# The scan's input products from a stack of 96 rows: one fp32r pass each in place of full fp32

## The reference, cut to what matters

```python
h = rms_norm(x, attn_norm_g[i])
proj = h @ w_in[i] + b_in[i]
q, k, v, u, gate_attn, gate_ssm = jnp.split(proj, SPLIT_POINTS, axis=-1)
...
ug = u.reshape(bsz, l, SSM_GROUPS, SSM_GROUP)          # 32 groups of 16 channels
...
bu_re = jnp.einsum('gph,blgh->blgp', bb_re, ug)        # 64 states of each group
bu_im = jnp.einsum('gph,blgh->blgp', bb_im, ug)
...
_, _, xs_re, xs_im = lax.associative_scan(combine, (a_re_t, a_im_t, bu_re, bu_im), axis=1)
y = (jnp.einsum('ghp,blgp->blgh', c_re, xs_re) - jnp.einsum('ghp,blgp->blgh', c_im, xs_im)
     + d_skip.reshape(SSM_GROUPS, SSM_GROUP) * ug)
```

## Time and profile before

| | |
|---|---|
| time before, median of 3 runs | 2671.86 us (2671.49 to 2672.24) |
| profiled execution, span from first to last instruction | 2672.7 us |
| PE busy | 2642.9 us (99%) |
| DVE busy | 1804.4 us (68%) |
| ACT busy | 1274.7 us (48%) |
| POOL busy | 249.9 us (9%) |
| granted TensorE clock, mean over the span | 0.995 |

### The profile page before, as it was taken

The page is one execution under the profiler, slowest core; times in us unless marked ns, Lnnn a source line. Parts: engine busy times, 40 slices in busy tenths (PEclk is TensorE's granted clock), DMA queues, the critical chain, the costliest instruction groups (busy, mean ns, idle before and its releaser), DMA issues.

```text
span 2672.7 us, 57540 instructions
## 1 busy us (share of the span) xinstructions
PE 2642.9 (99%) x22834; PEld 2628.9 (98%) x22834; DVE 1804.4 (68%) x2269; ACT 1274.7 (48%) x1548; POOL 249.9 (9%) x206
## 2 busy tenths in 40 slices
PE   9999999999999999999999999999999999999998
PEld 9999999999999999999999999999999999999998
DVE  5455555747888888864467999867576777775444
ACT  5334455345344444444455556554455555554442
POOL 1000000030000000001101665400100000000000
PEclk9999999999999999999999999999999999999999
DMA  7665556574555655556656555556656666666664
GB/s 256 193 199 175 150 161 182 169 213 148 173 195 196 196 194 189 196 191 203 192 168 200 174 163 157 155 183 200 194 183 195 196 194 193 191 190 197 195 191 141
DMA packets 137806, 496.71 MB, mean 186 GB/s; under 512 B 15425, under 2 KB 15425, under 8 KB 137537
## 3 DMA queue, kind: packets, MB, share of 16 engines
q1 hardware_dynamic: 137520, 494.20, 59.7%
q10 hardware_dynamic: 144, 0.52, 0.1%
HBM read 492.57 MB, written 2.10 MB: 185 GB/s over the span
## 4 chain that ended last, share of the span: by engine, by line
PE 89%; DVE 6%; DVEq 2%; ACT 1%; DMA 1%; issue 1%; ACTq 0%; SPq 0%
PE bank L432 86%; DVE w_lo L982 2%; PE ps_a L432 1%; PE ps_o L432 1%; PE ps_n L432 1%; DVE act_lo L1021 1%; PE ps_t L432 0%; DMA hT<-in_xT 0%; ACT w_hi L676 0%; DMA w_raw<-in_w_in 0%; ACT act_hi L742 0%; DVE hT L1046 0%; DVE pr L1309 0%; DVE rstd L1005 0%; DVEq L1299 0%
## 5 line engine op out<-in xcount | busy, mean ns | idle before, releaser
L982 DVE TENSOR_TENSOR w_lo<-w_raw,w_hi 128x1024 fp32r<-128x1024 f32 x928 | 1134.1, 1234 | 720.8 <-ACT w_hi L676 719.2
L676 ACT ACTIVATE w_hi<-w_raw 128x1024 fp32r<-128x1024 f32 x928 | 977.0, 1056 | 1185.9 <-PE bank L432 1045.3
L432 PE MATMUL bank<-act_hi,w_hi 128*128 128x256 f32 x5408 | 1275.3, 279 | 3.0 <-DVE gate_y L1350 2.5
L432 PE MATMUL bank<-act_lo,w_hi 128*128 128x256 f32 x5408 | 1264.9, 277 | 0.0
L432 PEld LDWEIGHTS bank<-act_hi,w_hi 128*128 128x128 f32 x5408 | 1014.9, 188 | 4.1 <-issue 2.7
L432 PEld LDWEIGHTS bank<-act_lo,w_hi 128*128 128x128 f32 x5408 | 1015.7, 188 | 0.7
L432 PE MATMUL bank<-act_hi,w_lo 128*128 128x256 f32 x5408 | 726.9, 277 | 2.7 <-DVE w_lo L982 2.7
L432 PEld LDWEIGHTS bank<-act_hi,w_lo 128*128 128x128 f32 x5408 | 666.6, 188 | 3.1 <-DVE w_lo L982 3.1
L432 PE MATMUL bank<-f_lo,w_hi 128*128 128x256 f32 x1408 | 327.9, 276 | 0.0
L432 PE MATMUL bank<-f_hi,w_hi 128*128 128x256 f32 x1408 | 327.9, 276 | 0.0
L432 PEld LDWEIGHTS bank<-f_lo,w_hi 128*128 128x128 f32 x1408 | 264.3, 188 | 0.0
(11 more groups left out here) (227 smaller groups left out, 1790.3 us busy)
## 6 DMA issues: line engine op xcount, KB each, us to landing
w_raw<-in_w_up SPq DMA_DIRECT2D x352, 512.0 KB, 4.2
w_raw<-in_w_in SPq DMA_DIRECT2D x252, 512.0 KB, 4.2
w_raw<-in_w_down SPq DMA_DIRECT2D x176, 512.0 KB, 4.2
w_raw<-in_w_out SPq DMA_DIRECT2D x64, 512.0 KB, 4.4
w_raw<-in_w_ple_gate SPq DMA_DIRECT2D x32, 512.0 KB, 4.5
w_raw<-in_w_branch_attn SPq DMA_DIRECT2D x16, 512.0 KB, 3.9
w_raw<-in_w_branch_a SPq DMA_DIRECT2D x8, 512.0 KB, 4.1
w_raw<-in_w_branch_b SPq DMA_DIRECT2D x8, 512.0 KB, 3.5
```

Of the source, the lines that this page charges most:

```text
L432: return pe.matmul(o, l, r, start=start, stop=stop, skip_group_check=True)
L676: act.activation(w_hi[:, k, 0:n, :], w_raw[:, k, 0:n, :], ACT.Copy).then_inc(hi_ready, 1)
L982: dve.tensor_tensor(w_lo[:, k, 0:n, :], w_raw[:, k, 0:n, :], w_hi[:, k, 0:n, :].bitcast(F32), ALU.subtract).then_inc(lo_ready, 1)
```

## The change

The products of a scan tile have 32 rows that are not zero. The host now lays B's 32 rows three times into bc_pad, at partitions 0, 32 and 64, with nothing below. Three DMAs issued by ACT bring the 32 channels of u to the same three places of u_raw. ACT rounds both to fp32r into stack, 96 rows of B and 96 of u. DVE then replaces the rows of B from 64 and the rows of u from 32 by what rounding took off. So the 96 rows hold high, high and low B beside high, low and high u, and one fp32r product over 96 rows gives the three partial sums that a piece's products also use. C and everything behind the products stays.

Where this stands is set by three new place functions. The fetch (at_fetch) of tiles 0 and 1 is behind ACT's piece 10, of later ones behind piece max(13, 4n+4). The rounding on ACT and the subtractions on DVE (at_stack) are behind their pieces 11 and 13 for tiles 0 and 1, then 4n+7. PE's products (at_input) are behind piece 10 and 14 for tiles 0 and 1, then 4n+8 as before. The queues of SP and POOL hold what they held.

```diff
--- before.py
+++ after.py
@@ -61,6 +61,10 @@
 at_stick = lambda h: 43 + 6 * h
 at_state = lambda n: 8 + 4 * n
 at_head = lambda h: 22 + 3 * h
+
+at_fetch = lambda n: 10 if n < 2 else max(13, 4 * n + 4)
+at_stack = lambda n: (11, 13)[n] if n < 2 else 4 * n + 7
+at_input = lambda n: (10, 14)[n] if n < 2 else at_state(n)
 
 
 def which(place, count, n):
@@ -226,6 +230,8 @@
         pT2_buf = tab[:, 0:BLK]
         vtok = tab[:, 2 * BLK:2 * BLK + T].rearrange("p (k c) -> p k c", k=2)
         turn_t = tab[:, 2 * BLK + T:2 * BLK + 3 * T].rearrange("p (k t) -> p k t", k=2)
+
+        stack, u_raw = over(40 * T, ("stack", [P, 2, 4 * P], F32R), ("u_raw", [P, 2, T]))
 
         x2_hi, x2_lo, glu_v, glu_g = over(
             PROJ2 * T, ("x2_hi", [P, 16, T], F32R), ("x2_lo", [P, 16, T], F32R), ("glu_v", [P, 4, T]), ("glu_g", [P, 4, T]))
@@ -270,6 +276,8 @@
         turns_ready, rot_ready, out_scaled = sem("turns_ready"), sem("rot_ready"), sem("out_scaled")
         negated = sem("negated")
         scans_ready, x_im_ready = sem("scans_ready"), sem("x_im_ready")
+        u_landed = [sem(f"u_landed{i}") for i in range(2)]
+        stack_rounded, stack_ready = sem("stack_rounded"), sem("stack_ready")
         v_ready, v_read, x_ready, x_used = sem("v_ready"), sem("v_read"), sem("x_ready"), sem("x_used")
         y_kept, y_act, ple_used = sem("y_kept"), sem("y_act"), sem("ple_used")
         stored = sem("stored")
@@ -586,16 +594,13 @@
             def mixer_2(n):
                 if n == 3:
                     sum_squares(4)
-                for m in which(at_state, STATE_TILES, n):
-
-                    if m % 8 == 0:
-                        pe.wait_ge(biased_ready, m // 8 + 1)
-                    pe.wait_ge(bc_landed[m % STATE_RING], 16 * (m // STATE_RING + 1))
+                for m in which(at_input, STATE_TILES, n):
+                    pe.wait_ge(stack_ready, m + 1)
                     if m >= 2:
                         pe.wait_ge(v_read, m - 1)
-                    u = proj2[:, U2 + m // STATE_BLOCK, :]
-                    mm(ps_a[m % 2][:, 0:TOK], bc_pad[:, m % STATE_RING, 0, :], u, True, True)
-                    mm(ps_a[m % 2][:, TOK:], bc_pad[:, m % STATE_RING, 1, :], u, False, True).then_inc(v_ready, 1)
+                    u = stack[0:96, m % 2, 2 * P:]
+                    mm(ps_a[m % 2][:, 0:TOK], stack[0:96, m % 2, 0:P], u, True, True)
+                    mm(ps_a[m % 2][:, TOK:], stack[0:96, m % 2, P:2 * P], u, False, True).then_inc(v_ready, 1)
                 for m in which(lambda m: at_state(m) + 6, STATE_TILES, n):
                     k = m % STATE_BLOCK
                     if k == 0 and m:
@@ -832,6 +837,22 @@
                 if n == 7:
                     root(4)
                     act.preload_act_table(ACT.Exp)
+                for m in which(at_fetch, STATE_TILES, n):
+                    act.wait_ge(biased_ready, m // 8 + 1)
+                    if m >= 2:
+                        act.wait_ge(stack_ready, m - 1)
+                    rows = slice(32 * (m % STATE_BLOCK), 32 * (m % STATE_BLOCK) + 32)
+                    for j in range(3):
+                        act.dma_start(u_raw[32 * j:32 * j + 32, m % 2, :], proj2[rows, U2 + m // STATE_BLOCK, :]
+                                      ).then_inc(u_landed[m % 2], 16)
+                for m in which(at_stack, STATE_TILES, n):
+                    act.wait_ge(bc_landed[m % STATE_RING], 16 * (m // STATE_RING + 1))
+                    if m >= 2:
+                        act.wait_ge(v_ready, m - 1)
+                    act.activation(stack[0:96, m % 2, 0:2 * P].rearrange("p (i s) -> p i s", i=2),
+                                   bc_pad[0:96, m % STATE_RING, 0:2, :], ACT.Copy)
+                    act.wait_ge(u_landed[m % 2], 48 * (m // 2 + 1))
+                    act.activation(stack[0:96, m % 2, 2 * P:], u_raw[0:96, m % 2, :], ACT.Copy).then_inc(stack_rounded, 1)
                 for m in which(lambda m: at_state(m) + LEAD - 1, STATE_TILES, n):
                     if m == 0:
                         act.wait_ge(turns_ready, 1)
@@ -1228,6 +1249,11 @@
                     root(4)
                 if n in (4, 5):
                     turn_tables(n - 4)
+                for m in which(at_stack, STATE_TILES, n):
+                    dve.wait_ge(stack_rounded, m + 1)
+                    b, u = stack[64:96, m % 2, 0:2 * P].rearrange("p (i s) -> p i s", i=2), stack[32:64, m % 2, 2 * P:]
+                    dve.tensor_tensor(b, bc_pad[64:96, m % STATE_RING, 0:2, :], b.bitcast(F32), ALU.subtract)
+                    dve.tensor_tensor(u, u_raw[32:64, m % 2, :], u.bitcast(F32), ALU.subtract).then_inc(stack_ready, 1)
                 for step in range(3):
                     for m in which(lambda m: at_state(m) + LEAD + step, STATE_TILES, n):
                         state_tile(m, step)
@@ -1663,7 +1689,8 @@
         vb, vc = np.asarray(v[f"ssm_b_{part}_2"])[0], np.asarray(v[f"ssm_c_{part}_2"])[0]
         for g in range(32):
             ch, st = slice(16 * (g % 8), 16 * (g % 8) + 16), slice(64 * (g % 2), 64 * (g % 2) + 64)
-            bc[ch, g // 2, i, st] = vb[g].T
+            for j in range(3):
+                bc[32 * j + 16 * (g % 2):32 * j + 16 * (g % 2) + 16, g // 2, i, st] = vb[g].T
             bc[st, g // 2, 2 + i, ch] = vc[g].T
     return bc
 
```

## The result

The changed kernel takes 2697.28 us (median of 4 runs, 2695.41 to 2699.28) against 2671.68 for the kernel before (4 runs beside it). The ratio is 1.0097 with a 95% interval from 1.0084 to 1.011, so it is 25.6 us slower. The forecast was 2686.3, 14.6 us slower by that median, in a range from 2675 to 2699. The direction and the engine were right.

A forecast was written before the change was run, and what follows sets the result against it. DVE's queue was taken to set the stage's end up to 1570.66, PE the pace behind it. First tile 2.4 plus pairs 16.5 less room 4.5 gave 14.4 us on 2672.7; less 0.8, 2686.3, range 2675 to 2699.

The forecast's parts named there:

- DVE's queue sets the end: Second block's input projection: up to 1570.66, whatever DVE does later than now is lost one for one.
- The first tile, 2.4 us: Tile 0's fetch and rounding on ACT delay piece 12's high half, so DVE starts its low half 2.4 us late.
- 15 pairs at 1.1 us: Two added DVE subtractions in each of tiles 1 to 15, at 1.1 us a tile: 16.5 us.
- DVE's room of 4.5 us: DVE's spare time behind 1570.66: 3.2 us of waits plus 1.3 of lead gained, taken off the added work.
- PE's saving pays nothing: The 10.1 us saved on PE's input products over 16 tiles only lengthen its waits.
- The range: Whole kernel, for 8 in 10: 2675 to 2699 us, leaving out the fast rival and reaching the slow one.
- ACT late: Rival: fetch and rounding on ACT delay DVE at seven places, 13 us more, 2699; chance 0.15.
- PE sets the time: Rival: the four-piece ring hides DVE's additions and PE's saved 10.1 us pay, 2661.8; chance 0.08.
- It cancels: Rival: bare subtractions and no first wait, +5.7 us or a little less, about 2677, within 0.2%; chance 0.09.
- Subtractions from 0.4 to 1.0 us: Sign: profile rows of the new DVE subtractions should read 0.4 to 1.0 us each.
- No waits of DVE for high halves behind piece 20: Sign: past piece 20 of the stage, DVE should no longer wait for ACT's rounded high halves.
- The three-tile period of 45.27: Sign: three scan tiles, 1585.31 to 1630.58 before, take 45.27 us; the prediction is wrong if this shrinks.

The follow-up runs named there:

- e2: Kernel before with the two DVE subtractions per tile added at the change's places, result unread, old products, no fetch or rounding on ACT: 2695.78 us, ratio 1.0086.
- e4: Kernel before with only the input products replaced by short 96-row ones on a constant tile (not the reference's values): 2669.99 us, ratio 0.9989.
- e1: Changed kernel without DVE's subtractions, low parts left out, ACT's second rounding releasing PE: 2672.41 us against 2673.30, ratio 0.9999.
- e3: Kernel before with ACT's part added (48 DMAs, 32 roundings, unread), nothing added on DVE, old products: 2674.99 us, ratio 1.0008.
- e10: Whole change with fetch, rounding and subtractions two pieces earlier from tile 2 or 3 on: 2685.54 us against 2671.33 for the kernel before, ratio 1.0051.
- e5: Like e2, but the subtractions stand two pieces later in DVE's queue, ahead of the scans, where POOL waits: 2681.80 us against 2671.34, ratio 1.0037.
- e8: Changed kernel with the two subtractions on POOL instead of DVE, behind its rotation table of the same tile, with drains: 2680.78 us, ratio 1.0036.
- e12: Change moved as in e10, SP issuing the fetches, DVE's kpad and vpad copies on ACT and their memsets on POOL: 2681.09 us, ratio 1.0038.
- e6: Like e2, at the same place, but with all operands of the subtractions at partitions 0 to 31: 2694.70 us, ratio 1.0084.

## Why the prediction was right in sign and wrong in size

**DVE's queue sets the end.** Right, and stronger than said. The window table (idle 15.9 and 16.8), e2 and e4 show it.

**The first tile, 2.4 us.** Measured 1.9 at tile 0 in the changed kernel, and 1.9 in e1 and e3. The low half of piece 12 starts at 1489.10; counted from the stage's start that is 1.9 later than in the earlier trace rows. The size is near and the reason was in part wrong. The prediction had ACT waiting for the copies to land. ACT's timeline of the changed kernel shows the rounding of u right behind that of B, with no wait:

```profile
1484.97 1.06 ACT L681 ACTIVATE w_hi<-w_raw 128x1024 fp32r<-128x1024 f32 x1 [3.02 <-issue]
...
1486.24 0.40 ACT L855 ACTIVATE stack<-u_raw 96x256 fp32r<-96x256 f32 x1
...
1488.03 1.04 ACT L681 ACTIVATE w_hi<-w_raw 128x1024 fp32r<-128x1024 f32 x1
```

Counted from the stage's start (2.3 earlier here), the high half of piece 11 is 1.3 later than in the earlier trace rows, the six issues having taken 3.84 us where 2.47 (6 x 0.411) were put; the two roundings add 0.6. The copies landed in a median of 2.7 where 3.5 was put, and that cost nothing. That the sum came out near is luck: issues that were too short stood beside a landing that was too long.

**15 pairs at 1.1 us.** This is the term that was mis-sized. By starts the pairs cost 25.0, 1.67 each, and by their rows 990 + 926 ns = 1.92 in the mean of all 16. The 25.0 are what is left after 1.9 us of DVE's waits were taken up, and the sum counts those waits in another term, the room. So the price to set against 1.1 is (25.0 + 1.9) / 15 = 1.79. The two ends, 0.68 and 1.9, held it. I took the middle between two net prices of the copies, and those copies have one SBUF input each. The nearest row by kind was L1309, two SBUF inputs, which goes from 1044 to 1646 at 512 columns. Its stretch of 0.6 us on each of the two subtractions would have given 0.68 + 1.2 = 1.9. The mis-sizing is 26.9 - 16.5 = 10.4.

**DVE's room of 4.5 us.** Nearly right in size: 1.9 of waits taken up and 2.1 of lead used are 4.0, 0.5 less than put, which the first tile gave back. So the forecast's 2.4 + 16.5 - 4.5 = 14.4 is to be read as 1.9 + 26.9 - 4.0 = 24.8. How the room was read was wrong. "Behind 1570.66 PE sets the pace and DVE follows": in e4 PE is faster and DVE moves by no more than 0.2 at any tile. PE without a gap for 140 us meant only that it ran just behind DVE's releases. And not every wait of an engine is room. The prediction took 3.2 of the 3.4 us of the earlier trace rows as such, but in the changed kernel, with DVE over 20 us later at the end, four waits of 0.5 are still there.

**PE's saving pays nothing.** Right within the change: the 2.1 come off in e2, which has no short products, just as in the change. Alone, in e4, 2.0 us of it arrive by starts.

**The range.** 2697.28 lies in it by luck. The forecast's own mechanism was given 2678 to 2694, and the measured time is 3.3 us above that. The range reached to 2699 for the sake of the ACT rival, which e3 refutes; the time came so near to that rival's 2699 because the pairs cost more.

**ACT late** (0.15): refuted by e3, where a tile costs nothing. **PE sets the time** (0.08): refuted by the result and by e4. **It cancels** (0.09): refuted by the result; even the best place that was tried for the whole change, e10, is 0.5% slower.

**What was to be seen.** PE's gaps over 20 us: 28.9. Two products of normal length: yes. The low half of piece 12 about 2 us late: 1.9. Subtractions from 0.4 to 1.0 us: the first of a pair is 1.16 in the median, so this sign pointed at the mis-sized term. No waits of DVE for high halves behind piece 20: wrong, 2.0 us remain from 1535 on. The stages before and after to 0.5 us: those after, to 0.1 (24.8 - 2.3 and the span's 22.6); the start of the stage moves from execution to execution. The three-tile period of 45.27, which was not to shrink, is 48.59 (input products of tiles 7 and 10, at 1596.22 and 1644.81).

## What to carry to other kernels

Where two engines are nearly full, count idle time, not busy time, in the stage, and look one step behind a wait before calling it room: here half of DVE's waits were still there when DVE got 25 us more work. Price a small DVE operation with two SBUF inputs by its kind, from the nearest two-input row beside POOL, before its shape; then look for a place in its queue where POOL is idle, since the place was worth 14 of 26 us by starts in e5 and 11.7 us for the whole change in e10. A cheaper product is worth little (2.0 of 11.0 us here) while it waits for an engine that is late already, and less than nothing if that engine has to prepare its operands.

## What the runs showed of the hardware

- A subtraction of 32x256 with two SBUF inputs takes 417 ns on DVE with POOL idle. The first of a pair takes 1159 and 1163 in the median at the change's place, mostly beside POOL (the changed kernel and e2), the second 864 and 868. The product that reads PSUM, 691/692/693 ns in the changed kernel, shows nothing of POOL. The same subtractions on POOL take 715 to 1560 ns (e8).
- A product over 96 rows runs at the rate of one over 128: both take about 0.28 us with their end and start 0.12 apart (287 ns in the median, two in 0.41 us).
- A DMA issued from ACT held its queue 612 ns in the median (514 to 839, 48 of them). Issued from SP in e12, such a fetch took 582 ns in the median. The copies of 32 rows within SBUF landed in 1.8 to 4.6 us.
- Two subtractions that follow each other with all operands at partitions 0 to 31 start 0.33 us apart away from POOL (e6), with operands at 64 and then at 32 0.43 (e2).
- PE's clock fell behind its idle stretches. After the wait of 3.89 us that ended at 1546.92, the windows show it, and again behind the one of 2.89 that ended at 1580.20:

```profile
1546.00:1549.00 3.00, 2.08 (x8) 1.90 (x9) 2.83 (x6) 0.31 (x2) 2.41 (x4) 0.70 0.52 205
1549.00:1552.00 3.00, 3.00 (x22) 3.00 (x21) 2.92 (x4) 2.81 (x6) 3.00 (x4) 0.74 0.44 85
1581.00:1584.00 3.00, 3.00 (x18) 3.00 (x17) 2.97 (x2) 1.60 (x3) 2.86 (x3) 0.55 0.69 236
1667.00:1670.00 3.00, 3.00 (x16) 3.00 (x16) 2.74 (x6) 1.75 (x3) 3.00 (x4) 0.50 0.27 108
```

The third such stretch holds a window whole: a granted clock of 0.50 is the lower level, 1.2 GHz; from 1664 to 1667 PE was busy 1.00 of 3.00 us. Products start 0.21 us apart there and 0.12 at the upper one. In the kernel before, the windows of the stage are at 1.00. What these stretches cost by themselves was not measured. They are a likely part of why PE's busy time fell by 4.7 us and not by e4's 11.0; in e2, which has old products and the pairs, it rose by 2.6 (2642.9 to 2645.5).
